# Two-layer gated trunk: the first merge gate by seven block products, attention after every second short job, probabilities scaled on ScalarE

## The reference

```python
h = rms_norm(x, norm_g[l])
proj = jnp.einsum('bsd,de->bse', h, w_in[l])
(a_u, a_v, a_z, b_q, b_k, b_v, b_z, i_q, i_k, i_w, g_a, g_b) = split_columns(proj)
y_a = spatial_gating_branch(gelu(a_u), gelu(a_v), a_z, ...)      # branch A, 512 wide
att = sparse_attention_branch(q, k, v, qi, ki, i_w, topk)        # branch B, 4 heads, 128 keys of up to 512
y_b = att * jax.nn.silu(b_z)
o_a = jnp.einsum('bse,ed->bsd', y_a, w_oa[l])
o_b = jnp.einsum('bse,ed->bsd', y_b, w_ob[l])
merged = jax.nn.sigmoid(g_a + gate_b[l, 0]) * o_a + jax.nn.sigmoid(g_b + gate_b[l, 1]) * o_b
x = x + jnp.einsum('bsd,de->bse', merged, w_out[l])
```

## Time and profile before

| | |
|---|---|
| median of 3 runs | 789.74 us (789.71 to 791.07) |
| the profiled execution | 789.07 us, its span 786.9 us |
| PE busy | 776.5 us (99%) |
| DVE busy | 617.9 us (79%) |
| ACT busy | 393.2 us (50%) |
| POOL busy | 152.0 us (19%) |
| granted clock of PE | 0.998 of full speed |

### The profile page before, as it was taken

The page is one execution under the profiler, slowest core; times in us unless marked ns, Lnnn a source line. Parts: engine busy times, 40 slices in busy tenths (PEclk is TensorE's granted clock), DMA queues, the critical chain, the costliest instruction groups (busy, mean ns, idle before and its releaser), DMA issues.

```text
span 786.9 us, 11503 instructions
## 1 busy us (share of the span) xinstructions
PE 776.5 (99%) x4124; PEld 667.6 (85%) x4124; DVE 617.9 (79%) x1058; ACT 393.2 (50%) x718; POOL 152.0 (19%) x137
## 2 busy tenths in 40 slices
PE   7999999999999999999999999999999999999998
PEld 7988888888788889988899888888887888899886
DVE  5779999979767667769986799999786666656895
ACT  6576656341354336745564765543324434467242
POOL 1257511100010103012211674110000101120130
PEclk9999999999999999999999999999999999999999
DMA  9634238733264237785873532478222723397684
GB/s 333 221 120 123 79 107 167 155 107 107 80 161 96 67 80 114 201 260 111 193 234 108 166 84 73 134 155 194 76 85 87 181 82 55 79 160 257 146 145 124
DMA packets 51561, 108.38 MB, mean 138 GB/s; under 512 B 3376, under 2 KB 8688, under 8 KB 51504
## 3 DMA queue, kind: packets, MB, share of 16 engines
q0 software_dynamic: 18896, 39.93, 26.7%
q1 hardware_dynamic: 32320, 67.12, 26.6%
q10 hardware_dynamic: 288, 0.59, 0.2%
HBM read 90.85 MB, written 6.29 MB: 123 GB/s over the span
## 4 chain that ended last, share of the span: by engine, by line
PE 87%; DVE 10%; issue 1%; DMA 1%; ACT 1%; DVEq 0%; SPq 0%; ACTq 0%
PE bank L836 17%; PE bank L838 17%; PE bank L837 17%; PE bank L957 6%; PE bank L903 3%; PE bank L905 3%; PE bank L904 3%; PE bank L873 3%; PE bank L875 3%; PE bank L874 3%; PE bank L810 2%; PE bank L828 2%; DVE w_lo L1403 2%; PE bank L766 1%; PE bank L819 1%; PE bank L781 1%
## 5 line engine op out<-in xcount | busy, mean ns | idle before, releaser
L1403 DVE TENSOR_TENSOR w_lo<-w_raw,w_hi 128x1024 fp32r<-128x1024 f32 x144 | 186.5, 1310 | 11.2 <-ACT w_hi L1042 6.7
L1042 ACT ACTIVATE w_hi<-w_raw 128x1024 fp32r<-128x1024 f32 x144 | 148.2, 1054 | 21.4 <-DMA w_raw<-in_w_out 14.7
L836 PE MATMUL bank<-h_lo,w_hi 128*128 128x512 f32 x320 | 128.0, 400 | 0.0
L838 PE MATMUL bank<-h_hi,w_hi 128*128 128x512 f32 x320 | 124.8, 390 | 0.0
L837 PE MATMUL bank<-h_hi,w_lo 128*128 128x512 f32 x320 | 124.5, 389 | 0.0
L836 PE MATMUL bank<-w_lo,h_hi 128*128 128x512 f32 x256 | 100.5, 392 | 0.0
L838 PE MATMUL bank<-w_hi,h_hi 128*128 128x512 f32 x256 | 99.9, 390 | 0.0
L837 PE MATMUL bank<-w_hi,h_lo 128*128 128x512 f32 x256 | 99.8, 390 | 0.0
L838 PEld LDWEIGHTS bank<-h_hi,w_hi 128*128 128x128 f32 x320 | 60.0, 188 | 12.9
L836 PEld LDWEIGHTS bank<-h_lo,w_hi 128*128 128x128 f32 x320 | 60.1, 188 | 12.3
L837 PEld LDWEIGHTS bank<-h_hi,w_lo 128*128 128x128 f32 x320 | 60.1, 188 | 12.2
(11 more groups left out here) (206 smaller groups left out, 1731.7 us busy)
## 6 DMA issues: line engine op xcount, KB each, us to landing
w_raw<-in_w_in SPq DMA_DIRECT2D x92, 512.0 KB, 4.2
w_raw<-in_w_in POOLq DMA_DIRECT2D x16, 512.0 KB, 6.0
w_raw<-in_w_out POOLq DMA_DIRECT2D x16, 512.0 KB, 6.3
w_raw<-in_w_out SPq DMA_DIRECT2D x12, 512.0 KB, 4.2
out<-x_sb POOLq DMA_DIRECT2D x4, 1024.0 KB, 6.1
w_raw<-in_w_oa SPq DMA_DIRECT2D x8, 512.0 KB, 4.2
w_raw<-in_w_ob SPq DMA_DIRECT2D x8, 512.0 KB, 3.6
x_sb<-out POOLq DMA_DIRECT2D x2, 2048.0 KB, 10.9
```

What stands on the lines that cost most here:

```text
L836: nc.tensor.matmul(dst, s_h, m_l, start=(n == 0), stop=False)
L838: last = nc.tensor.matmul(dst, s_h, m_h, start=False, stop=(n == len(pairs) - 1))
L1042: nc.scalar.activation(hi, w_raw[:, raw_slot(layer, u)], ACT.Copy).then_inc(s_whi.sem, 1)
L1403: nc.vector.tensor_tensor(lo, w_raw[:, raw_slot(layer, u)], hi.bitcast(F32), ALU.subtract) \
```

## The change

The first gate, ga, becomes a group of 14 short jobs like gb, with the same sums of h, the first of which (s5) is therefore needed by GA[4] and no longer by GB[4]. The functions of the second gate take the gate as an argument (`gate_copied`, `gate_added`, `gate_tanh`, `gate_job_products`). The tables follow: where each unit of weights lives, in which bank a job of oa works, when each sum of h is made. The sum s4 is gathered in the lower half of `g_a` and no longer in `silu_um`. Attention calls stand after ZA[2], seven jobs of ga, four of oa and six of gb. The scaling of the probabilities moves from DVE to ACT; the reciprocal stays on DVE. In the diff ga has 14 units of weights (8 of them added by POOL) where it had 8 (two groups of four, all loaded by SP).

```diff
-    ("ga", "w_in", COL["ga"], 4), ("ga", "w_in", COL["ga"] + W512, 4),
+    ("ga", "w_in", COL["ga"], 14),
...
+OA_BANKS = [2, 6, 0, 1, 2, 0, 1, 6]
...
-_slots = list(range(JOB_ZA[2], JOB_GA[-1] + 1)) + JOB_OA[1::2] + JOB_GB[0:7:2]
+_slots = JOB_ZA[2:3] + JOB_GA[::2] + JOB_OA[::2] + JOB_GB[0:11:2]
...
-SPLIT_YB = {JOB_GB[8]: [0, 1], JOB_GB[9]: [2], JOB_GB[10]: [3]}
+SPLIT_YB = {JOB_GB[11]: [0, 1], JOB_GB[12]: [2], JOB_GB[13]: [3]}
...
-H_PARTS_AFTER = {JOB_VB[2]: 0, JOB_VB[3]: 1, JOB_VA[0]: 2, JOB_VA[1]: 3, JOB_VA[3]: 4, JOB_GA[1]: 5}
+H_PARTS_AFTER = {JOB_VB[2]: 0, JOB_VB[3]: 1, JOB_VA[0]: 2, JOB_VA[1]: 3, JOB_VA[3]: 4, JOB_ZA[1]: 5}
...
-H_HI_AFTER = {JOB_OA[1]: "s5", JOB_OA[5]: "s3", JOB_GB[2]: "s6", JOB_GB[3]: "s4"}
-H_LO_AFTER = {JOB_OA[3]: "s5", JOB_GB[0]: "s3", JOB_GB[3]: "s6", JOB_GB[5]: "s4"}
+H_HI_AFTER = {JOB_ZA[3]: "s5", JOB_GA[0]: "s3", JOB_GA[2]: "s6", JOB_GA[4]: "s4"}
+H_LO_AFTER = {JOB_GA[1]: "s5", JOB_GA[3]: "s3", JOB_GA[5]: "s6", JOB_GA[7]: "s4"}
...
-              23: [(2, 1), (3, 2)], 26: [(3, 1)], 28: [(3, 2)], 29: [(3, 1)], **{s: [(3, 2 if s in (34, 36) else 1)] for s in range(32, 40)}}
+              23: [(2, 1), (3, 1)], 24: [(3, 1)], 25: [(3, 1)], 33: [(3, 1)], 35: [(3, 1)], 37: [(3, 1)], 39: [(3, 1)],
+              41: [(3, 1)], 43: [(3, 1)], 45: [(3, 1)], 47: [(3, 2)], 49: [(3, 1)], 51: [(3, 2)], 53: [(3, 1)]}
...
-            return {"s5": h5_raw[:], "s3": h3_raw[:], "s6": h6_raw[:], "s4": h4_raw}[name]
+            return {"s5": h5_raw[:], "s3": h3_raw[:], "s6": h6_raw[:], "s4": bottom(g_a)}[name]
...
-                for u in range(GB_U, GB_U + SEVEN):
-                    if unit_adds(u):
-                        add_weights(u)
+                for g in (GA_G, GB_G):
+                    for u in range(UNIT_FIRST[g], UNIT_FIRST[g] + SEVEN):
+                        if unit_adds(u):
+                            add_weights(u)
...
                 act.wait_ge(s_hterm[name].sem, s_hterm[name].at(layer, 16 * H_TERMS[name]))
                 if name == "s5":
-                    act.wait_ge(s_job.sem, s_job.at(layer, JOB_GA[-1] + 1))
+                    act.wait_ge(s_job.sem, s_job.at(layer, JOB_ZA[-1] + 1))
                     act.wait_ge(s_hterm["s4"].sem, s_hterm["s4"].at(layer, 48))
...
                 if H_PARTS[i] == "-a11 hi to s4":
-                    act.wait_ge(s_ya.sem, s_ya.at(layer, A_GROUPS))
+                    act.wait_ge(s_mix.sem, s_mix.at(layer, A_GROUPS))
...
                         act.sem_inc(s_exp.sem, 1)
+                        act.wait_ge(s_rowinv.sem, s_rowinv.at(layer, i + 1))
+                        nc.scalar.activation(probs[:, i % 2, 0:w], probs[:, i % 2, 0:w], ACT.Copy,
+                                             scale=row_inv[:, i:i + 1]).then_inc(s_prob.sem, 1)
...
-            def attention_scale(layer, i):
-
-                w = P * (ATT_STEPS[i][1] + 1)
+            def attention_inverse(layer, i):
+
                 dve.wait_ge(s_exp.sem, s_exp.at(layer, i + 1))
-                vec.link(dve, nc.vector.reciprocal(row_inv[:, i:i + 1], row_sum[:, i:i + 1]))
-                nc.vector.tensor_scalar(probs[:, i % 2, 0:w], probs[:, i % 2, 0:w], row_inv[:, i:i + 1], None,
-                                        ALU.mult).then_inc(s_prob.sem, 1)
+                nc.vector.reciprocal(row_inv[:, i:i + 1], row_sum[:, i:i + 1]).then_inc(s_rowinv.sem, 1)
```

198 lines of the change are left out of this document (106 added, 92 removed).

## The result

The changed kernel takes **815.08 us** (median of 4 runs, 814.01 to 815.37) against 789.75 in the same session: ratio 1.0317, interval 1.0302 to 1.0333. The forecast was 807.2 with a range of 796 to 813: slower, as foretold, but by 25.3 us and not by 17.5, and 2 us outside the range.

A forecast was written before the change was run, and what follows sets the result against it. PE, busy 99% of the span, was taken as the bound. 789.07 less 8.2 of gains plus 2 x (6.7 + 5.5 + 0.6) gave 806.5, with 0.67 to the median 807.2 us; range 796 to 813.

The forecast's parts named there:

- The gain: Short jobs in ga save PE 3.2 us a layer; its first waits for scaled probabilities go; 8.2 us in all.
- The chain of s4: Start of ga: PE stands at attend(2) behind s4's DMAs, s5's rounding and weight additions; 6.7 us a layer.
- The clock: Rival, chance 0.2: PE's clock falls after the 6.7 us wait and queues lengthen, 2 to 3.5 us more a layer; about 812.5.
- the four times: Forecast 807.2 us; rivals: chain costs but load doesn't 796.2 (0.2), faster 781.5 (0.05), clock falls about 812.5 (0.2).
- DVE's load: In ga and oa DVE has no time left, so PE waits at GA[4], GA[6] and GA[12]; 5.5 us a layer.
- The end of gb: ob's first job waits for the last parts of yb, made behind GB[13]'s tanh; 0.6 us a layer.
- Faster: Rival, chance 0.05: ACT reaches s5's rounding after s4's last term, needing a chain under 11 us; 781.5 us.

The follow-up runs named there:

- before_scale_act: The kernel before with only the scaling of the probabilities moved from DVE to ACT; 790.01 us, ratio 1.0002.
- scale_dve: The changed kernel with the scaling of the probabilities put back on DVE; 817.91 us, ratio 1.0363.
- adds_first: The changed kernel with the two additions to s5's weights ahead of s4's third term on POOL's queue; 810.65 us, ratio 1.0279.
- ring4608: The changed kernel with 4608 instead of 4096 bytes of room for GpSimd's DMA descriptors; 813.99 us, ratio 1.0317.
- all_three_tk: all_three with one top-k round taken from GA[1] to oa; 792.65 us, ratio 1.0041.
- after_topk: The changed kernel with the top-k rounds of GA[3] and GA[5] put into oa; 813.85 us, ratio 1.0311.
- best_topk: adds_before with the top-k rounds of GA[3] and GA[5] put into oa too; 795.43 us, ratio 1.0071.
- adds_before: all_three_tk, with DVE in ga adding the bank before forming the slot's remainders, and s3 and s6 rounded one job later; 789.84 us, ratio 1.0007.
- inverse_behind_tk: inverse_behind with one more top-k round moved from GA[3] to GA[13]; 787.91 us, ratio 0.9978.
- part_early: The changed kernel with ACT's copy that starts s4's chain one job earlier, after ZA[0] instead of ZA[1]; 801.24 us, ratio 1.0153.
- all_three: The changed kernel with s4's copy one job earlier, s5's weight additions ahead of s4's third term, s5 rounded after GA[0]'s attention, s3 one job later; 793.28 us.
- inverse_behind: adds_before, with DVE forming s3's second remainder ahead of the inverse of the row sums, and ACT rounding s6 and s4 later; 790.26 us, ratio 1.0004.
- early_later: The changed kernel with s4's copy one job earlier and s5's two weight units rounded after ga's first attention step; 796.61 us, ratio 1.0087.
- units_later: The changed kernel with s5's two weight units rounded one job later, behind the attention of GA[0]; 809.70 us, ratio 1.0249.

## Why the prediction was wrong

**The gain: right.** Short jobs start 2.88 us apart (344.30 to 347.18), and the waits of 0.70 and 1.06 us at the first call went. It was the calls' new places that did it, as foretold, and not the scaling: by itself it leaves them (before_scale_act), and without it they are gone too (scale_dve).

**The chain of s4: right mechanism, term too small (6.7 us; 10.7 measured: 9.3 and 1.4).** This is the step that failed. The first half was near: ACT takes up the last term at 219.8 against 218.1, of which 0.2 is the later copy and 1.5 the chain's own length (18.9 us against 17.4), half a us more than I had allowed for the strided rows. The other half was not: of the two additions it says "they land at 219.4 and 220.6". They landed at about 222.3 and 225.9. I had given each its median landing of 6.0 us from its issue, as if they ran side by side with the third term and each other. The five transfers get in each other's way: the first addition, with the third term ahead of it, took 7.8 us, and all five took 24.6 us together (201.3 to 225.9), still 21.4 in adds_first, the best order tried. That POOL was held at the second addition (3.8 us, which I had not foreseen) cost 0.8 us: ring4608.

**The clock: it fell, was in no sum of the forecast, and cost almost nothing.** I had it as a rival, with GA[3]'s doubling hidden in GA[4]'s wait. So it was: the addition that frees GA[4]'s bank ended at 235.38, and GA[4] started 0.20 us behind it. At full speed PE would have waited 1.6 us there. In layer 1 the addition ended at 634.21 and GA[4] started at 634.61, so there the clock cost 0.2 us. The rival's "some 3 us at half speed" stood on no row; the clock read 0.50 for more than 6 us of work (228.2 to 234.7). Its 812.5 is the nearest of the four times, but by luck: what it added for the clock was hidden, and the missing time was in the additions.

**DVE's load: right places, only half the mechanism (5.5 us; 2.4 measured, 4.6 with the slow job and what is ahead of it).** The waits stand at GA[6] (0.8 and 0.6 against 0.8 and 1.0) and GA[12] (1.0 against 1.6), and the 2.1 of GA[4] are the 1.6 under the slow job. But DVE was busy 40.8 + 20.7 = 61.4 us in ga and oa, not 67.0, and idle for 21 of the 61.9 us of ga, 13.7 of them while it stood behind ACT up to 228.0; behind the stall it is busy 22.3 of 26 us (236 to 262). Taking load away from where DVE next waits for ACT only lengthens that wait (all_three_tk, after_topk, best_topk); another order removes waits of PE (adds_before), and so does a round taken from straight ahead of what PE wants (inverse_behind_tk). "DVE has no time left at all" was the false step: it had time, but not its turn.

With these terms the sum closes: 4.0 us a layer too little for the chain, 0.9 too much for the rest of ga, 0.2 too little in ob make 6.6 of the 7.9 us by which the forecast was short.

**The end of gb: right** (0.6; 0.5 of wait, 0.8 in all).

**"Faster"** (chance 0.05) was argued on the chain's length alone, with the start fixed. The start was not fixed: part_early moves it, and inverse_behind_tk is faster than the kernel before. It reaches 787.9 and not the 781.5 of that rival; its remaining waits in ga and gb and those in ob are 2.1 us of the difference in layer 0 and 2.9 in layer 1, and what the rest is no run tells apart.

What stays open: what decides whether the clock falls. It is not the length of the wait ahead of GA[4]: in all_three PE waits 1.92 us there in layer 0 and 1.91 in layer 1, and the clock falls only in layer 1; in all_three_tk, with the same two waits, only in layer 0. Nor is it the kernel: of the 12 executions of adds_before five have a mean clock of 1.000 (788.88 to 789.80 us) and two have 0.995 (791.57 and 791.72).

## What to carry to other kernels

Before moving work that needs a chain of transfers to an earlier place, move the chain's start by as much, and put everything that waits for a landing behind whatever the matrix engine wants next from that engine: one table entry was worth 13.8 us here, and order, with new slots for two rounds of the top-k, made a change that lost 3.2% win 0.2%. Price several transfers in flight by the time of all of them together, not each by its own median. And where two engines take turns (exponential, reciprocal, scaling), look first at what stands where: less load helped only straight ahead of what the matrix engine wants; ahead of a turn it lengthened the wait for the other engine.

## What the runs showed of the hardware

- An accumulating transfer of 512 KB landed 4.8 to 6.2 us after its issue with no other of POOL's in flight ahead of it (the terms of s4 in layer 0: 4.8 to 5.6 in the kernel before, 5.5 to 6.2 in the changed one), and after 7.8 to 12.9 beside others (first addition of the changed kernel 7.8, third term of adds_first 7.9 and of adds_before 11.7, second addition of adds_before 12.9). The Trainium skill, "DMA: Bandwidth & Descriptors", section "Anatomy of one DMA — SWDGE (gpsimd) path", gives 2.0 us and the bytes by 436 GB/s; by it 512 KB land in 3.2 us, an estimate. No accumulating transfer of this size in any run here took less than 4.5 from issue to landing.
- GpSimd stood 3.8 us at one issue with no releaser named, the second addition behind the third term, and 3.6 to 4.5 at the same place in the other runs with that order; 4608 bytes of descriptor space in place of 4096 took that away wholly, and 0.8 us of PE's wait with it.
- The granted clock fell to its lower level during the wait of 9.3 us (changed kernel) and near the end of that of 2.7 (part_early), and behind one of 1.9 (inverse_behind), but stayed at 1.00 after 1.9 and 1.2 (adds_before); behind the same wait of 1.9 it fell in one layer of all_three and not in the other. A short job cost 5.12 us start to start nearly all at the lower level (GA[3] in layer 1 of part_early), 3.02 at the upper.
- A bank that DVE's addition frees is taken up by PE 0.20 us after the addition's end, in each of the waits at GA[4] (early_later, units_later, all_three).
